# Expert rows of the last three steps added by marking matrices in numbers that differ per token tile, two more tiles read between the last two scatters

## The chip, the cores and the metric

The kernel runs on one core of a Trainium2 chip. A core has TensorE (matrix products, written PE in the profile, its weight loads PEld), VectorE (DVE), ScalarE (ACT), GpSimd (POOL) and SyncE (SP, which here issues most DMAs), and 16 DMA engines that all queues share. The metric is the device time of one execution in microseconds, lower is better.

## What is computed

One decoder layer on 1024 tokens of width 1024: a normalised and modulated input, two attention parts, an output projection, then a mixture of 32 experts in 4 groups, each token going to two experts of one group, and a last normalisation. Only the end matters here:

```python
hid = jax.nn.silu(jnp.dot(h, w_gate[e])) * jnp.dot(h, w_up[e])
y = y + gates[:, e:e + 1] * jnp.dot(hid, w_down[e])      # for every expert e
...
x = x + gate_m[:, None] * y
return rms_norm(x, g_final)
```

## The kernel before

**Expert steps.** Tokens chosen by experts are put on lists, and 20 steps (`NSTEP`) take 128 list entries each. In a step GpSimd gathers the 128 rows (`gather`, L753 on), TensorE turns them, multiplies them with the gate, up and down weights, and VectorE writes the weighted result rows into one of five buffers `held` (`ev_y`). GpSimd then scatters them (`scatter`, issued at L767) to the DRAM tensor `expert_rows` (`y_dram` in the code). It has two rows for each token, one for each of its two experts; one of the pair also carries the token's residual row. A list entry with a negative destination isn't written.

**Late steps.** The last three steps, 17, 18 and 19, are late (`NLATE`, `LATE` = 17). Of their rows, those of the tokens of tiles 0, 1 and 2 (`AHEAD`; a tile is 128 tokens) are not scattered: `late_dst` sets their destination to -1. They are added on TensorE instead. For each of these three tiles and each late step there is a marking matrix (`marks`, 9 of 128 by 128, made by VectorE in expert steps 3 to 11 by comparing `iota_tok` with a column of `late_tok`): a one where list entry and token meet. `add_into` (L2222) multiplies it with the rows still held in `held` and adds into two PSUM banks of the tile; a last product with the identity adds the tile's rows that came by way of DRAM. One product of this kind, marking or identity, covers two halves of 512 columns; it is called a block below. So before, a tile of the three has three marking blocks and one identity block. Since tiles 0 to 2 may miss rows, SyncE first writes zeros to their rows of `expert_rows` (L550), early in the kernel.

**The tail.** SyncE reads both rows of each token back, two DMAs of 512 KB a tile (`expert_rows`, L617). Tiles 0, 1 and 2 are read when scatters 0 to 16 have landed. Tiles 3 to 7 (`read`) are read when all have (`rows_out`, set by GpSimd). VectorE adds the two halves: the early sums of tiles 0 to 2 at L1685, the others in `combine` (L1691), called sum 3 to sum 7. ScalarE squares the whole row of a tile and sums it (L1080, called square), out of PSUM for the tiles of `mixed` and out of SBUF for the others; GpSimd adds a small number (L826) and raises to the power -1/2 (L827); VectorE scales the tile by that and the final gain (`finish`, L1700, called scaling); SyncE stores it (L664). ScalarE, GpSimd and the stores follow the order `last`, tile 0, 3, 4, 1, 5, 6, 2, 7; VectorE's order is written out by hand at the end of its program.

Every engine executes its own instructions in the order in which they are written, and waits at semaphores. So an instruction that waits holds all that stands behind it on its engine.

Of the kernel before, what the change touches and what calls it, by code (L numbers as in the profile page):

```python
# [11 lines left out]
ALU = mybir.AluOpType  # L12
# [53 lines left out]
def hybrid_layer(nc, x, c, w_ada, b_ada, g_attn, w_in, g_kv, w_uk, w_uv, lam_q1, lam_k1, lam_q2, lam_k2,  # L66
# [88 lines left out]
    with ctx:  # L155
# [153 lines left out]
        def dist(t):  # L309
# [86 lines left out]
        late_tok = logits[:, :, :].rearrange("p t n -> p (t n)")[:, 2 * NT + 5 * T + NLATE:2 * NT + 5 * T + NLATE * (1 + AHEAD)].rearrange(  # L396
            "p (i j) -> p i j", j=NLATE)
# [63 lines left out]
        def scattered(b):  # L461

            return len(range(b, LATE, 2))
# [14 lines left out]
        def _(sp):  # L478
# [140 lines left out]
            for n in range(NSTEP + 1):  # L619
# [4 lines left out]
                if n >= 1:  # L624
# [16 lines left out]
            with sp.If(n_ov > 0):  # L641
# [12 lines left out]
                sp.wait_ge(yg_ahead, 64 * AHEAD)  # L654
# [14 lines left out]
        def _(pool):  # L669
# [132 lines left out]
            pool.wait_ge(yg_ahead, 32 * AHEAD)  # L802
# [5 lines left out]
            with pool.If(n_ov > 0):  # L808
# [3 lines left out]
                pool.wait_ge(y_last, 16 * NLATE)  # L812
# [8 lines left out]
            pool.wait_ge(y_last, 16 * NLATE)  # L821
# [9 lines left out]
        def _(act):  # L831
# [253 lines left out]
        def _(dve):  # L1085
# [566 lines left out]
            for n in range(NSTEP):  # L1652
# [9 lines left out]
                if 3 <= n < 3 + NLATE * AHEAD:  # L1662
# [593 lines left out]
```

## Time and profile before

| | us |
|---|---|
| median of 3 runs | 997.08 |
| lowest, highest | 996.19, 998.7 |
| the profiled execution | 995.87 |
| its span, first to last instruction | 994.1 |

| engine | busy us | share of the span |
|---|---|---|
| TensorE | 947.6 | 95% |
| VectorE | 630.1 | 63% |
| ScalarE | 398.3 | 40% |
| GpSimd | 120.3 | 12% |

The profile is of one execution. Times in its rows are counted from the start of the span. A row's busy time is that of the instruction, and the bracket behind it says how long its engine was idle before it and what ended that. The shares are averages over stages that are limited by different things: attention by TensorE, the expert steps by TensorE and the DMA engines together, the last 30 us by neither for their whole length. TensorE's granted clock was 0.992 of full speed over the span and 1.00 in the tail for as long as TensorE was busy there.

### The profile page before, as it was taken

What the parts mean: (1) busy time and instruction counts of PE and PEld (TensorE: products, weight loads), DVE (VectorE), ACT (ScalarE), POOL (GpSimd) and SP (SyncE); (2) the same over time, 40 slices, a digit from 0 to 9 for tenths busy, and PEclk for the clock granted to TensorE, in tenths of its full rate; (3) what the DMA queues carried; (4) which work ended last, traced back from release to release, by engine and by line L of the source; (5) the groups of instructions that cost most, each with busy time, mean ns of one, the idle gap of its engine ahead of it and who ended that gap; (6) DMA issues with size and microseconds to landing.
All of it is one profiled execution on the core that took longest, in us unless ns stands there. A gap on an engine that the chain in (4) does not pass through costs nothing.

```text
span 994.1 us, 15197 instructions
## 1 busy us (share of the span) xinstructions
PE 947.6 (95%) x5400; PEld 520.1 (52%) x5400; DVE 630.1 (63%) x1670; ACT 398.3 (40%) x901; POOL 120.3 (12%) x221
## 2 busy tenths in 40 slices
PE   3899999999999999999999999999899999999895
PEld 2455476444446856667776555555634433344342
DVE  3378646999999799887777423345724444444356
ACT  6131134676671188877668412121211221111103
POOL 2101000000005711110000000000111111111114
PEclk9899999999999999999999999999999999999998
DMA  9998100101103100040000410059899999999979
GB/s 324 328 358 298 43 22 22 44 21 43 43 22 107 69 1 1 2 171 23 2 2 1 156 57 37 27 212 404 312 411 421 393 423 420 420 420 421 420 307 372
DMA packets 70093, 188.37 MB, mean 189 GB/s; under 512 B 10280, under 2 KB 37216, under 8 KB 57728
## 3 DMA queue, kind: packets, MB, share of 16 engines
q1 hardware_dynamic: 61888, 169.48, 44.6%
q0 software_dynamic: 5760, 16.33, 4.2%
q10 hardware_dynamic: 2368, 1.57, 0.5%
q8 instruction: 44, 0.72, 0.3%
q14 instruction: 33, 0.27, 0.1%
HBM read 169.98 MB, written 22.04 MB: 193 GB/s over the span
## 4 chain that ended last, share of the span: by engine, by line
PE 53%; DVE 20%; DMA 16%; issue 6%; POOL 3%; ACT 1%; SPq 0%; DVEq 0%; POOLq 0%; ACTq 0%
DMA expert_rows<-HT,SC 12%; PE PS L2018 11%; DVE BIAS L1222 8%; PE PS L1911 6%; PE PS L2148 5%; PE PS L1954 5%; PE PS L1976 4%; PE PS L1872 3%; PE PS L2171 3%; PE PS L1824 3%; PE PS L1971 2%; DVE X L1286 2%; PE PS L1849 2%; PE PS L1789 2%; DMA HT<-h_rows,SC 2%
## 5 line engine op out<-in xcount | busy, mean ns | idle before, releaser
L1824 PE MATMUL PS<-HT,X 128*128 128x512 f32 x384 | 168.8, 593 | 0.0
L1824 PEld LDWEIGHTS PS<-HT,X 128*128 128x128 f32 x384 | 72.5, 190 | 92.4 <-issue 92.2
L936 ACT ACTIVATE X<-X,nmx 128x128 f32<-128x128 f32 (+7 forms) x128 | 98.4, 770 | 51.7 <-DVE nmx L1286 51.4
L2018 PE MATMUL PS<-QKV,HT 128*128 128x512 f32 x256 | 113.7, 597 | 0.0
L1222 DVE TENSOR_SCALAR_CACHE_REDUCE BIAS<-SC,W 128x384 f32<-128x384 f32 (+3 forms) x128 | 96.4, 810 | 1.1
L2148 PE MATMUL PS<-QKV,HT 128*32 128x512 f32 (+1 forms) x528 | 91.9, 594 | 2.8 <-ACT HT L1034 1.2
L919 ACT ACTIVATE X<-SC,W 128x896 f32<-128x896 f32 x64 | 69.6, 1088 | 43.1 <-DVE W L1210 43.1
L1594 DVE TENSOR_TENSOR HT<-PS,HT 128x256 f32<-128x256 f32 x20 | 8.5, 425 | 123.3 <-ACT HT L1042 123.3
L1911 PE MATMUL PS<-QKV 64*128 64x512 f32 (+3 forms) x384 | 79.0, 517 | 1.6 <-DVE nmx L1286 1.1
L2018 PEld LDWEIGHTS PS<-QKV,HT 128*128 128x128 f32 x256 | 47.4, 190 | 53.7 <-issue 53.6
L1954 PE MATMUL PS<-ident,X 128*128 128x128 f32 x432 | 63.2, 279 | 2.2 <-DVE X L1304 2.1
L1042 ACT ACTIVATE HT<-PS 128x256 f32<-128x256 f32 x20 | 7.7, 383 | 132.2 <-PE PS L2148 125.5
L1286 DVE CUSTOM_DVE_ANT_0 X<-PS,R 128x128 f32<-128x128 f32 (+7 forms) x80 | 50.8, 674 | 14.6 <-PE PS L1911 8.6
L2148 PE MATMUL PS<-SC,HT 128*32 128x512 f32 (+1 forms) x160 | 56.4, 593 | 0.0
L1286 DVE CUSTOM_DVE_ANT_0 X<-PS,SC 128x1024 f32<-128x1024 f32 (+5 forms) x48 | 42.0, 887 | 17.9 <-PE PS L1911 17.8
L1954 PEld LDWEIGHTS PS<-ident,X 128*128 128x128 f32 x432 | 47.3, 141 | 11.4 <-issue 8.6
L1911 PEld LDWEIGHTS PS<-QKV 64*128 64x128 f32 x384 | 31.6, 185 | 27.8 <-issue 20.6
L2148 PEld LDWEIGHTS PS<-QKV,HT 128*32 128x32 f32 (+1 forms) x528 | 24.6, 111 | 36.9 <-issue 34.0
L760 POOL DMA_INDIRECT HT<-h_rows,SC x20 | 20.6, 1029 | 188.9 <-DMA expert_rows<-HT,SC 132.2
L1114 DVE SCALAR_TENSOR_TENSOR QKV<-QKV,cact 128x512 f32<-128x512 f32 x56 | 42.1, 752 | 2.0
L1971 PEld LDWEIGHTS PS<-QKV,HT 128*128 128x128 f32 x288 | 34.5, 191 | 16.6 <-issue 9.2
L2148 PE MATMUL PS<-X,HT 128*32 128x512 f32 (+1 forms) x112 | 42.3, 593 | 0.0
(335 smaller groups left out, 1590.4 us busy)
## 6 DMA issues: line engine op xcount, KB each, us to landing
QKV<-in_w_down_dram SPq DMA_DIRECT2D x20, 1024.0 KB, 26.4
QKV<-in_w_gate_dram SPq DMA_DIRECT2D x19, 1024.0 KB
QKV<-in_w_up_dram SPq DMA_DIRECT2D x19, 1024.0 KB
QKV<-in_w_ada_dram SPq DMA_DIRECT2D x8, 2048.0 KB, 12.7
QKV<-in_w_ada_dram SPq DMA_DIRECT2D x8, 1024.0 KB, 12.5
X<-in_w_in_dram SPq DMA_DIRECT2D x16, 512.0 KB, 3.8
X<-in_w_down_dram SPq DMA_DIRECT2D x8, 1024.0 KB
W<-in_w_gate_dram SPq DMA_DIRECT2D x5, 1024.0 KB
```

What stands on the lines that cost most here:

```text
L919: act.activation(RL[:, n % 2, 0:w], SC[:, sc_off[t]:sc_off[t] + w], ACT.Sign, bias=tk[:, 4, i:i + 1].bitcast(F32), scale=-1.0, accum_out=c ...
L936: act.activation(sc, sc, ACT.Exp, bias=nmx[:, i % 4, m:m + 1], scale=-1.0, accum_out=rs[:, i, m:m + 1]).then_inc(exp_done, 1)
L1114: link(dve.scalar_tensor_tensor(out=w[:, 0, :], in0=w[:, j, :], scalar=cact[:, j:j + 1], in1=w[:, 0, :], op0=ALU.mult, op1=ALU.add))
L1222: dve.tensor_scalar(BIAS[:, i % 3, 0:w], SC[:, sc_off[t]:sc_off[t] + w], thr.bitcast(F32)[:, i:i + 1], 0.0, ALU.is_lt, ALU.add, accum_out= ...
L1286: dve.tensor_tensor_reduce(sc_buf[i % 4][:, m, 0:w], PS[:, 2 * m:2 * m + 2, :].rearrange("p a n -> p (a n)")[:, BANK * n:BANK * n + w], aw ...
L1824: end = pe.matmul(PS[:, 2 * b + half, :], WS[:, b, j, :], HT[:, j, BANK * half:BANK * (half + 1)], start=(j == 0), stop=(j == KC - 1))
L1911: end = pe.matmul(PS[:, 2 * m + n + c0 // BANK, 0:c1 - c0], QKV[rows_m, q0:q0 + P], QKV[rows_m, k0 + c0:k0 + c1], start=True, stop=True)
L1954: end = pe.transpose(PS[:, 4 + g % 2, c0:c0 + P], sc_buf[i % 4][:, m, P * b:P * (b + 1)], ident[:, :])
L1971: end = pe.matmul(PS[:, 6 + h % 2, slot], turned_at(i)[:, g % 4, P * (b - b0):P * (b - b0 + 1)], vf[:, u * S + P * b:u * S + P * (b + 1)], ...
L1976: end = pe.matmul(PS[DH * m:DH * (m + 1), 6 + h % 2, slot], vd[:, b, v0:v0 + DH], turned_at(i)[:, g % 4, c0:c0 + P], start=(b == 0), stop= ...
L2018: end = pe.matmul(PS[:, n % 4, :], HT[:, k, P * (n // 2):P * (n // 2 + 1)], wo[:, k, BANK * (n % 2):BANK * (n % 2 + 1)], start=(k == 0), s ...
L2148: end = pe.matmul(PS[at, 2 + b, :], hgT[b][:, P * c_ + at.start:P * c_ + at.stop], WGU[w][:, c_, :, :], start=(c_ == 0), stop=(c_ == KC - 1))
```

## The change

The three late steps are no longer treated alike. `first_late` = (0, 1, 1, 2, 2) says for tiles 0 to 4 from which late step on their rows are added by marking matrices. Tile 0 has three matrices, tiles 1 and 2 have two, tiles 3 and 4 have one: nine in all, as before. The rows that a matrix no longer covers are scattered: step 17 now leaves out tile 0 alone, step 18 tiles 0 to 2, step 19 tiles 0 to 4. What is read when changes with it: tile 0 after scatter 16, tiles 1 and 2 after scatter 17, tiles 3 and 4 after scatter 18, tiles 5 to 7 after scatter 19. Tiles 3 and 4 are now summed by VectorE first and then enter PSUM through an identity block, and are squared and scaled from PSUM. There are four pairs of banks for five tiles, so tile 4 reuses those of tile 0 and waits until tile 0 is scaled. Five tiles are zeroed at the start. The order of the tail on ScalarE, GpSimd and the stores is tile 0, 5, 1, 3, 6, 4, 7, 2.

```diff
-        AHEAD, NLATE = 3, 3
+        AHEAD, NLATE, PATCHED = 3, 3, 5
+        first_late = (0, 1, 1, 2, 2)
         LATE = NSTEP - NLATE
         read = (3, 4, 5, 6, 7)
-        last = (0, 3, 4, 1, 5, 6, 2, 7)
-        mixed = (0, 1, 2)
+        last = (0, 5, 1, 3, 6, 4, 7, 2)
+        mixed = (0, 1, 3, 4, 2)
...
-        marks = [mark_room[NLATE * i:NLATE * (i + 1)] for i in range(AHEAD)]
+        mark_of = [(i, j) for i in range(PATCHED) for j in range(first_late[i], NLATE)]
+        marks = {at: room for at, room in zip(mark_of, mark_room)}
+        tok_col = [mark_of.index((i, first_late[i])) for i in range(PATCHED)]
+        tiles_of = [sum(1 for f in first_late if f <= j) for j in range(NLATE)]
+        mix_banks = [2 * (i % 4) for i in range(PATCHED)]
...
-            for t in range(AHEAD):
+            for t in range(PATCHED):
                 for k in range(2):
                     row = S * k + P * t
                     sp.dma_start(y_dram[row:row + P, :], zero_rows).then_inc(yg_ahead, 16)
...
                     if n == LATE:
                         for b in range(2):
-                            sp.wait_ge(y_out[b], 16 * scattered(b))
+                            sp.wait_ge(y_out[b], 16 * len(range(b, LATE, 2)))
                         for t in range(AHEAD):
-                            expert_rows(t, yg_ahead)
+                            if first_late[t] == 0:
+                                expert_rows(t, yg_ahead)
+                    if n == LATE + 1:
+                        sp.wait_ge(y_out[1], 16 * scattered(1))
+                        for t in range(AHEAD):
+                            if first_late[t] == 1:
+                                expert_rows(t, yg_ahead)
...
             sp.sem_inc(tables_set, 1)
+            sp.wait_ge(y_out[0], 16 * scattered(0))
+            for t in range(AHEAD, PATCHED):
+                expert_rows(t, yg_in[read.index(t)])
             sp.wait_ge(rows_out, 1)
-            for i, t in enumerate(read):
-                expert_rows(t, yg_in[i])
+            for t in range(PATCHED, T):
+                expert_rows(t, yg_in[read.index(t)])
...
             def scatter(n):
 
                 pool.wait_ge(y_sb, 2 * n + 2)
+                if LATE <= n < NSTEP - 1:
+                    pool.wait_ge(y_out[n % 2], 16 * (n // 2))
...
-            link(dve.tensor_scalar(late_dst, PS[:, 2, LATE:NSTEP], P * AHEAD + 0.5, None, ALU.is_ge))
+            for j in range(NLATE):
+                link(dve.tensor_scalar(late_dst[:, j:j + 1], PS[:, 2, LATE + j:LATE + j + 1], P * tiles_of[j] + 0.5, None,
+                                       ALU.is_ge))
...
-            link(dve.tensor_copy(late_tok[:, 0, :], PS[:, 2, LATE:NSTEP]))
-            for i in range(1, AHEAD):
-                link(dve.tensor_scalar(late_tok[:, i, :], PS[:, 2, LATE:NSTEP], float(-P * i), None, ALU.add))
+            for i, f in enumerate(first_late):
+                link(dve.tensor_scalar(late_tok[:, tok_col[i]:tok_col[i] + NLATE - f], PS[:, 2, LATE + f:NSTEP], float(-P * i),
+                                       None, ALU.add))
...
             finish(0)
             combine(3)
             combine(4)
-            finish(3)
             combine(5)
-            finish(4)
+            finish(5)
             finish(1)
             combine(6)
-            finish(5)
+            finish(3)
+            finish(6)
             combine(7)
-            finish(6)
+            finish(4)
+            finish(7)
             finish(2)
-            finish(7)
...
-            for i in range(AHEAD):
-                for j in range(NLATE):
-                    pe.wait_ge(marked, NLATE * i + j + 1)
+            pe.wait_ge(marked, len(mark_of))
+            for t in mixed:
+                if t >= 4:
+                    pe.wait_ge(fin_done, last.index(t - 4) + 1)
+                for j in range(first_late[t], NLATE):
                     pe.wait_ge(y_sb, 2 * (LATE + j + 1))
-                    add_into(i, marks[i][j], held[(LATE + j) % HELD], j == 0, False)
-                pe.wait_ge(marked, NLATE * AHEAD + i + 1)
-                add_into(i, ident[:, :], yg[i][0], False, True).then_inc(mix_ps, 1)
+                    add_into(mix_banks[t], marks[(t, j)], held[(LATE + j) % HELD], j == first_late[t], False)
+                if t < AHEAD:
+                    pe.wait_ge(marked, len(mark_of) + t + 1)
+                else:
+                    pe.wait_ge(cb_done, read.index(t) + 1)
+                add_into(mix_banks[t], ident[:, :], yg[t][0], False, True).then_inc(mix_ps, 1)
```

VectorE at the end of its program, before the change, from scaling 0 on. L1700 is a scaling, L1691 a sum; X holds tiles 0 to 2, QKV tiles 3 to 7, PS is PSUM, yg_in0 to yg_in4 are the landings of tiles 3 to 7:

```order
L1700 SCALAR_TENSOR_TENSOR X<-PS,ss,HT 128x1024 [waits rstd_done,act_in]
L1691 TENSOR_TENSOR QKV<-QKV 128x1024 [waits yg_in0]
L1691 TENSOR_TENSOR QKV<-QKV 128x1024 [waits yg_in1]
L1700 SCALAR_TENSOR_TENSOR QKV<-QKV,ss,HT 128x1024 [waits rstd_done]
L1691 TENSOR_TENSOR QKV<-QKV 128x1024 [waits yg_in2]
L1700 SCALAR_TENSOR_TENSOR QKV<-QKV,ss,HT 128x1024 [waits rstd_done]
L1700 SCALAR_TENSOR_TENSOR X<-PS,ss,HT 128x1024 [waits rstd_done]
L1691 TENSOR_TENSOR QKV<-QKV 128x1024 [waits yg_in3]
L1700 SCALAR_TENSOR_TENSOR QKV<-QKV,ss,HT 128x1024 [waits rstd_done]
L1691 TENSOR_TENSOR QKV<-QKV 128x1024 [waits yg_in4]
L1700 SCALAR_TENSOR_TENSOR QKV<-QKV,ss,HT 128x1024 [waits rstd_done]
```

Two more scalings follow, of tile 2 and tile 7. The same place after the change, up to the scaling of tile 6; here L1717 is a scaling and L1709 a sum:

```order
L1717 SCALAR_TENSOR_TENSOR X<-PS,ss,HT 128x1024 [waits rstd_done,act_in]
L1709 TENSOR_TENSOR QKV<-QKV 128x1024 [waits yg_in0]
L1709 TENSOR_TENSOR QKV<-QKV 128x1024 [waits yg_in1]
L1709 TENSOR_TENSOR QKV<-QKV 128x1024 [waits yg_in2]
L1717 SCALAR_TENSOR_TENSOR QKV<-QKV,ss,HT 128x1024 [waits rstd_done]
L1717 SCALAR_TENSOR_TENSOR X<-PS,ss,HT 128x1024 [waits rstd_done]
L1709 TENSOR_TENSOR QKV<-QKV 128x1024 [waits yg_in3]
L1717 SCALAR_TENSOR_TENSOR QKV<-PS,ss,HT 128x1024 [waits rstd_done]
L1717 SCALAR_TENSOR_TENSOR QKV<-QKV,ss,HT 128x1024 [waits rstd_done]
```

Sum 7 and the scalings of tiles 4, 7 and 2 follow. Sum 5 moved in front of every scaling but that of tile 0, and its scaling stands directly behind it; tile 3 is scaled from PSUM, between sum 6 and the scaling of tile 6.

SyncE's queue from the last weight load to the first store, before the change (L450 is a weight load, L617 a read of a tile, L664 a store; the branch that is taken only when lists overflow is left out):

```order
L450 DMA QKV<-in_w_down_dram 128x2048
L617 DMA X<-expert_rows 128x1024 [waits dn_ps,y_out0,gu_ps,y_out1]
L617 DMA X<-expert_rows 128x1024 x5
...
L617 DMA QKV<-expert_rows 128x1024 [waits rows_out]
L617 DMA QKV<-expert_rows 128x1024 x9
L664 DMA out_0_dram<-X 128x1024 [waits fin_done]
```

And after it, where L622 is a read of a tile and L678 a store:

```order
L622 DMA X<-expert_rows 128x1024 [waits dn_ps,y_out0,gu_ps,y_out1]
L622 DMA X<-expert_rows 128x1024
L622 DMA X<-expert_rows 128x1024 [waits y_out1,dn_ps,gu_ps]
L622 DMA X<-expert_rows 128x1024 x3
...
L622 DMA QKV<-expert_rows 128x1024 [waits y_out0]
L622 DMA QKV<-expert_rows 128x1024 x3
L622 DMA QKV<-expert_rows 128x1024 [waits rows_out]
L622 DMA QKV<-expert_rows 128x1024 x5
L678 DMA out_0_dram<-X 128x1024 [waits fin_done]
```

Sixteen reads in two groups became sixteen reads in four: two, four, four and six.

## Rows read from the trace of the kernel before

**Rows 1.** Chain of waits, 930 to 995: start us, us, what.

```profile
963.82 3.35 DMA expert_rows<-HT,SC
...
967.32 0.33 SPq L617
...
968.64 6.20 DMA QKV<-expert_rows
```

**Rows 2.** Windows of 3 us: busy us of each engine, PEclk, DMA share, GB/s.

```profile
963.00:966.00 3.00, 3.00 (x8) 1.33 (x7) 2.15 (x3) 0.00 (x0) 0.97 (x1) 1.00 0.21 75
```

**Rows 3.** Timeline of the tail: start us, us, engine, line, operation [idle before].

```profile
963.89 3.50 DVE L1685 TENSOR_TENSOR X<-X 128x1024 f32<-128x1024 f32 x3 [0.85 <-issue]
...
969.57 0.19 POOL L826 TENSOR_TENSOR ss<-ss,eps_row 128x1 f32<-128x1 f32 x1 [4.77 <-ACT HT L1080]
...
970.50 1.28 DVE L1700 SCALAR_TENSOR_TENSOR X<-PS,ss,HT 128x1024 f32<-128x1024 f32 x1 [3.11 <-POOL ss L827]
...
972.30 1.23 DVE L1691 TENSOR_TENSOR QKV<-QKV 128x1024 f32<-128x1024 f32 x1 [0.52 <-DMA QKV<-expert_rows]
...
973.56 1.06 ACT L1080 ACTIVATE HT<-QKV 128x1024 f32<-128x1024 f32 x1 [4.08 <-DVE QKV L1691]
...
974.79 0.19 POOL L826 TENSOR_TENSOR ss<-ss,eps_row 128x1 f32<-128x1 f32 x1 [4.39 <-ACT HT L1080]
974.87 1.23 DVE L1691 TENSOR_TENSOR QKV<-QKV 128x1024 f32<-128x1024 f32 x1 [1.33 <-DMA QKV<-expert_rows]
...
975.06 1.45 POOL L827 TENSOR_TENSOR ss<-ss,neghalf 128x1 f32<-128x1 f32 x1
...
976.54 1.28 DVE L1700 SCALAR_TENSOR_TENSOR QKV<-QKV,ss,HT 128x1024 f32<-128x1024 f32 x1 [0.45 <-POOL ss L827]
...
981.12 1.28 DVE L1700 SCALAR_TENSOR_TENSOR X<-PS,ss,HT 128x1024 f32<-128x1024 f32 x1 [0.44 <-POOL ss L827]
981.32 0.54 POOL L827 TENSOR_TENSOR ss<-ss,neghalf 128x1 f32<-128x1 f32 x1
982.32 1.22 DVE L1691 TENSOR_TENSOR QKV<-QKV 128x1024 f32<-128x1024 f32 x1
...
984.65 1.22 DVE L1691 TENSOR_TENSOR QKV<-QKV 128x1024 f32<-128x1024 f32 x1
...
984.79 1.12 POOL L826 TENSOR_TENSOR ss<-ss,eps_row 128x1 f32<-128x1 f32 x1 [2.94 <-ACT HT L1080]
...
990.80 0.33 SPq L664 DMA_DIRECT2D out_dram<-QKV  x1
```

**Rows 4.** Timeline of TensorE, its marking blocks and the first identity block.

```profile
961.30 5.31 PE L2222 MATMUL PS<-HT,BIAS 128*128 128x512 f32 x12
...
966.45 1.88 PE L2222 MATMUL PS<-X,ident 128*128 128x512 f32 x4
```

**Rows 5.** Timeline of GpSimd, scatters 17 and 18.

```profile
948.38 0.97 POOL L767 DMA_INDIRECT expert_rows<-HT,SC  x1 [13.06 <-DVE HT L1606]
959.24 0.97 POOL L767 DMA_INDIRECT expert_rows<-HT,SC  x1 [9.89 <-DVE HT L1606]
```

**Rows 6.** The tile expert_rows at 948.3 to 948.45, scatter 17 alone.

```profile
DMA to landing us min/median/max: 7.7/7.7/7.7
```

**Rows 7.** The tile expert_rows at 959 to 960, scatter 18 alone.

```profile
DMA to landing us min/median/max: 5.0/5.0/5.0
```

**Rows 8.** The tile expert_rows, SyncE, 948 to 952: the six early reads.

```profile
L617 SPq DMA_DIRECT2D X<-expert_rows x6: 319/458/509, 948.5 to 951.1; - x6
...
DMA to landing us min/median/max: 6.0/8.1/11.0
```

**Rows 9.** The tile expert_rows, SyncE, 969.6 to 970: both reads of tile 5.

```profile
DMA to landing us min/median/max: 7.0/7.3/7.5
```

**Rows 10.** Timeline of VectorE before the first expert step, 713 to 716.

```profile
715.74 0.41 DVE L1616 TENSOR_SCALAR HT<-PS,gm,modc 128x128 f32<-128x128 f32 x1 [1.91 <-PE PS L2135]
```

**Rows 11.** The tile expert_rows over the span: the zeroing stores.

```profile
L550 SPq DMA_DIRECT2D expert_rows<-W x6: 433/1188/1596, 317.3 to 322.7; - x6
```

More of the change, by code:

```diff
@@ L461, in scattered @@
         def scattered(b):
-            return len(range(b, LATE, 2))
+            return len(range(b, NSTEP - 1, 2))
         def uses(b):
@@ L653, in _ @@
                 sp.wait_ge(rows_out, 1)
-                sp.wait_ge(yg_ahead, 64 * AHEAD)
+                sp.wait_ge(yg_ahead, 32 * PATCHED + 32 * AHEAD)
                 for t in range(AHEAD):
@@ L769, in scatter @@
                                         bounds_check=2 * S - 1, oob_is_err=False
-                                        ).then_inc(y_out[n % 2] if n < LATE else y_last, 16)
+                                        ).then_inc(y_out[n % 2] if n < NSTEP - 1 else y_last, 16)
             def overflow_rows(n, i, b):
@@ L801, in _ @@
             pool.wait_ge(route_done, 2)
-            pool.wait_ge(yg_ahead, 32 * AHEAD)
+            pool.wait_ge(yg_ahead, 32 * PATCHED)
             for n in range(NSTEP):
@@ L811, in _ @@
                     pool.wait_ge(y_out[b], 16 * scattered(b))
-                pool.wait_ge(y_last, 16 * NLATE)
+                pool.wait_ge(y_last, 16)
                 with pool.Fori(0, NOV // 2) as i:
@@ L820, in _ @@
                 pool.wait_ge(y_out[b], 16 * scattered(b))
-            pool.wait_ge(y_last, 16 * NLATE)
+            pool.wait_ge(y_last, 16)
             pool.sem_inc(rows_out, 1)
@@ L1073, in _ @@
                     act.wait_ge(mix_ps, i + 1)
-                    whole = PS[:, 2 * i:2 * i + 2, :].rearrange("p a n -> p (a n)")
+                    whole = PS[:, mix_banks[t]:mix_banks[t] + 2, :].rearrange("p a n -> p (a n)")
                 else:
@@ L1661, in _ @@
                     dve.wait_ge(tables_set, 2 * NE + 2)
-                if 3 <= n < 3 + NLATE * AHEAD:
-                    i, j = divmod(n - 3, NLATE)
-                    dve.tensor_scalar(marks[i][j], iota_tok, late_tok[:, i, j:j + 1], None, ALU.is_equal).then_inc(marked, 1)
+                if 3 <= n < 3 + len(mark_of):
+                    dve.tensor_scalar(marks[mark_of[n - 3]], iota_tok, late_tok[:, n - 3:n - 2], None,
+                                      ALU.is_equal).then_inc(marked, 1)
             dve.wait_ge(route_done, 2)
@@ L1669, in _ @@
                     dve.wait_ge(y_out[b], 16 * scattered(b))
-                dve.wait_ge(y_last, 16 * NLATE)
+                dve.wait_ge(y_last, 16)
                 place_overflow()
@@ L1682, in _ @@
             dve.wait_ge(tables_set, 2 * NE + 3)
-            dve.wait_ge(yg_ahead, 64 * AHEAD)
+            dve.wait_ge(yg_ahead, 32 * PATCHED + 32 * AHEAD)
             for t in range(AHEAD):
@@ L1696, in finish @@
                 if t in mixed:
-                    i = mixed.index(t)
-                    whole = PS[:, 2 * i:2 * i + 2, :].rearrange("p a n -> p (a n)")
+                    whole = PS[:, mix_banks[t]:mix_banks[t] + 2, :].rearrange("p a n -> p (a n)")
                 dve.wait_ge(rstd_done, rstd_out + last.index(t) + 1)
@@ L2217, in _, with add_into @@
                             down_proj(n, over(b), [(b, 0, 4)], [(b, came(DNS))])
-            def add_into(i, stationary, rows, start, stop):
+            def add_into(bank, stationary, rows, start, stop):
                 for h in range(2):
-                    end = pe.matmul(PS[:, 2 * i + h, :], stationary, rows[:, BANK * h:BANK * (h + 1)], start=start,
+                    end = pe.matmul(PS[:, bank + h, :], stationary, rows[:, BANK * h:BANK * (h + 1)], start=start,
                                      stop=stop)
                 return end
-            for i in range(AHEAD):
-                for j in range(NLATE):
-                    pe.wait_ge(marked, NLATE * i + j + 1)
-                    pe.wait_ge(y_sb, 2 * (LATE + j + 1))
-                    add_into(i, marks[i][j], held[(LATE + j) % HELD], j == 0, False)
-                pe.wait_ge(marked, NLATE * AHEAD + i + 1)
-                add_into(i, ident[:, :], yg[i][0], False, True).then_inc(mix_ps, 1)
+            pe.wait_ge(marked, len(mark_of))
[3 more added lines that the diff above has]
+                for j in range(first_late[t], NLATE):
+                    pe.wait_ge(y_sb, 2 * (LATE + j + 1))
+                    add_into(mix_banks[t], marks[(t, j)], held[(LATE + j) % HELD], j == first_late[t], False)
[4 more added lines that the diff above has]
+                add_into(mix_banks[t], ident[:, :], yg[t][0], False, True).then_inc(mix_ps, 1)
 _INS = ["x", "c", "w_ada", "b_ada", "g_attn", "w_in", "g_kv", "w_uk", "w_uv", "lam_q1", "lam_k1", "lam_q2", "lam_k2",
```

4 lines of the change are left out of this document (2 added, 2 removed).

## Prediction

> **What bounds the kernel now.** I read the page first, then the chain of waits, the DMA by windows, and the timeline of the last 35 us. Only the tail is touched in a way that can move the end, so the reader should see three things there. First, the last scatter (step 19) is issued at 963.82 and its landing, 3.35 us later, starts all ten reads of tiles 3 to 7; the read issued at 968.64 lands 6.20 us later and only then does tile 4's sum start [rows 1]. Second, the DMA engines are nearly idle at 963 to 966 (share 0.21) [rows 2]: that hole is where the change puts four reads. Third, around 981 to 985 VectorE runs without a gap: sums (1.22 us each) and final scalings (1.28 us) stand back to back, and the last store is issued at 990.80 [rows 3]. TensorE's adding, 12 blocks that begin at 961.30 [rows 4], ends at about 982, long before the end. So the reads bound the tail until about 977, VectorE with its partners after that.
>
> **What the change removes: waiting for tiles 3 and 4.** Scatters 17, 18, 19 landed 7.7, 5.0 and 3.4 us after their issues at 948.38, 959.24 and 963.82, so at 956.1, 964.2 and 967.2 [rows 1, 5, 6, 7]. Tiles 1 and 2 are now read when scatter 17 has landed. At 956.1 at the latest, four reads start; by the spacing of the ten reads before (first issue 967.32, the fourth, of 968.64, landed at 974.84, which is 7.5 us) they land by 963.6, where the six early reads of before ended at 951.1 + 11.0 = 962.1 [rows 1, 8]. VectorE's first early sum starts at 963.89 anyway, takes 1.17 us, and TensorE wants it at 966.45 [rows 3, 4], so 1.4 us are spare: between 0 and 0.5 us of delay, and I take none.
> The queue in front of scatter 18 empties those 1.5 us later, so it lands not at 964.2 but between 964.2 and 965.7; I take 965.2, nearer to the late end because the load of the final gain and the scatter itself share that queue time. Four reads are then issued from 965.2, against 967.32 before: 2.1 us earlier, not the 4.6 us that lie between the two scatters. The engines have the hole of [rows 2] for them, and tiles 5 to 7 follow in the same stream. Tile 5's second read, issued at 969.9, landed 7.5 us later at 977.4, 10.1 us after the first issue [rows 9]; now 965.2 + 10.1 = 975.3.
>
> **What it adds on TensorE.** Nine marking blocks stay nine; identity blocks grow from 3 to 5. A block is 4 matmul instructions of 0.43 us (12 from 961.30 to 966.45) [rows 4], 1.72 us. Two more are 3.4 us; 14 blocks from 961.30 end at 985.4. The order is now tile 0, 1, 3, 4, 2, and the new waits (the sum of tile 3, the first scaled tile, the sum of tile 4) are over by 974, before TensorE comes to them at 975 or later. Behind the last block come square, power and scaling: 985.4 + 0.2 + 1.2 + 0.9 + 1.3 = 989.0. That is a floor, 1.8 us under 990.8.
>
> **What it moves: the order on VectorE, ScalarE and GpSimd.** This is the term that decides. Before, each scaling of a summed tile had at least one other VectorE instruction between it and its sum; now scaling 5 stands right behind sum 5, scaling 1 behind it, and so on. Durations: a sum lets its square start 1.25 us after its own start, the square feeds GpSimd 1.23 us later (973.56 to 974.79), and GpSimd's two small instructions need 0.93 us when nothing holds them (969.57 to scaling 0 at 970.50) [rows 3]. They are held: the power that started at 975.06 took 1.45 us and ended 0.41 us after the sum that began at 974.87; the one at 981.32, beside a scaling that reads PSUM, took only 0.54 us; the addition at 984.79, beside a sum, 1.12 us [rows 3]. Back to back, a scaling costs 1.20 (981.12 to 982.32), a sum and a scaling together 2.33 (982.32 to 984.65), so a sum 1.13 [rows 3].
> With sum 5 starting at S: it ends S+1.2; scaling 5 can start only at S+1.25+1.23+0.93 = S+3.4, so VectorE idles 2.2 us. Power 1 is held by scaling 5, so scaling 1 starts at S+5.1. Sum 6 S+6.3; scaling 3 (from PSUM) S+7.5, ends S+8.7; square 6 is behind sum 6, so scaling 6 starts S+6.3+3.4 = S+9.7, idle 1.0. Sum 7 S+10.9. Power 4 is held by scaling 6 and sum 7, so scaling 4 starts S+12.6; scaling 7 at S+10.9+3.4 = S+14.3; power 2 is held by scaling 7, so scaling 2 starts S+16.3 and ends S+17.6. Tiles 6 and 7 have landed long before their sums.
> S itself: scaling 0 is unchanged at 970.50 [rows 3], sums 3 and 4 follow at 971.7 and 972.8, so S is at least 974.0 by VectorE; by the reads it is 975.3. The end on VectorE is 975.3 + 17.6 = 992.9, against 990.8: **+2.1 us**. The gain of 2.1 us at the reads is spent by some 5 us of new idle places and by a chain of four tiles behind sum 6. With S = 974.0 it is 991.6, +0.8 us.
> The Trainium skill, SBUF — State Buffer, section A bandwidth-pool intuition that's wrong, says that the held engine goes on some 115 ns after VectorE's end, where the power here ended 0.41 us after it. By the page the sum would be about 0.3 us smaller.
>
> **Edits that cost nothing.** Four more short VectorE instructions before the first expert step, 0.2 us each or 0.8 us: VectorE waited 1.91 us there for TensorE, up to 715.74 [rows 10]; without that cover they cost 0.8 us. Four more zeroing stores of 512 KB at about 323: six took 317.3 to 322.7 to issue [rows 11], so some 5 us more of SyncE's queue, whose next entry waits for the end of all scores, hundreds of us away. GpSimd's new waits before scatters 17 and 18 are for scatters 15 and 16, which SyncE also awaits before its early reads; those began right after 948.38, so the waits are over when they come. What is queued behind them, scatter 19 and the small instructions of the tail, isn't moved.
>
> **Rivals.** (a) *The last scatter is held by the reads in front of it (slower).* The four reads share the DMA engines with scatter 19. For: scatter 17, with six reads beside it, took 7.7 us, scatter 19, alone, 3.4 [rows 1, 6]. If it takes 7.7 now it lands at 971.5, tile 5 follows 5.0 us later (as tile 3 did, 972.30 after 967.32) [rows 1, 3], S = 976.6, the end 994.2: +3.4 us, 1000.5. It costs something from a landing after 970.2, and decides the sign at 0.3% from about 971. Against: its rows flow at about 965 to 966, before the data of reads issued at 965.2, and fewer rows (tiles 5 to 7 only) are written.
> The Trainium skill, DMA: Bandwidth & Descriptors, section Queues, rings and completion order, has each DMA engine take turns between queues packet by packet. By that rule scatter 19 would share with the reads and end nearer this rival.
> (b) *The early reads carry through (faster).* If the idle places do not open, because the squares and powers return faster than the rows say, the end falls to TensorE's floor: 989.0, -1.8 us, 995.3. For it speaks that VectorE's busy work is no larger than before. Against it: 3.4 us from sum to scaling is seen in the trace (972.30 and 976.54, 4.2 with a held power) [rows 3].
> (c) *The change doesn't do what it says.* Scatter 18, behind the later reads of tiles 1 and 2, lands no earlier than scatter 19 does. Then S is 977.4 as before and the end 995.0, +4.2 us, 1001.3. It needs a latency of 8 us where 5.0 was seen.
>
> **How the numbers follow.** The profiled execution took 995.87 with a span of 994.1; the median of the runs is 997.08, 1.2 above it, and I add the change to the median: 997.08 + 2.0 = 999.1. A measurement can tell about 0.3%, 3 us, from no change. Chances: forecast, S between 974.0 and 976.1 (+0.8 to +2.9), 0.68; rival (a) 0.18; rival (b) 0.09; rival (c) 0.05. Rival (b) alone stays within 3 us save for a small part, so faster 0.02, same 0.75, slower 0.23. The range runs from +0.1 (the forecast's low end less what a median scatters) to +3.9 us, so 997.2 to 1001.0, and leaves out (b) and (c).
>
> **What would show it.** In the trace after: four reads issued near 965 instead of 967.3; sum 5 near 975.3; VectorE idle some 2 us behind sum 5 with GpSimd as its releaser, and again 1 us before scaling 6; TensorE ending near 985.4 with no wait; the last scaling ending near 993. I am wrong if scatter 19 lands after 970, if the early sums start after 965.2, or if scaling 5 starts less than 3 us after sum 5.

## The result and the profile after

The changed kernel takes 999.97 us (median of 15 runs, 997.89 to 1002.94), the kernel before, run beside it, 995.28 us (15 runs, 990.93 to 998.7). The ratio is 1.0054, 95% interval 1.0041 to 1.0067: 5.3 us slower. A second series of the same kernel, run later beside the kernel before, gave 1.0051 (1.0038 to 1.0064, 5 runs). The profiled execution took 999.74 us with a span of 998.0.

Where the last 35 us begin differs by some microseconds from one execution to the next: TensorE's first marking block starts between 959.2 and 963.5 in the traces kept here, at 959.96 and at 963.49 in two of the changed kernel. So all places in the tail are counted here from that event, at 961.30 before [rows 4] and at 959.96 after. Before, the last store is issued 29.5 us behind it [rows 3], after it 35.0 us behind it. By these two traces that is 5.5 us, so the whole loss lies in this stretch.

The chain of waits of the changed kernel (start us, us, what) answers to [rows 1]:

```profile
957.90 8.53 DMA expert_rows<-HT,SC
...
966.44 0.33 SPq L622
...
969.11 8.13 DMA QKV<-expert_rows
...
977.26 1.24 DVE QKV L1709
...
978.52 1.16 ACT HT L1096 x2
...
993.62 1.28 DVE X L1717
```

It is scatter 18, not scatter 19, that now starts the reads, and it took 8.53 us to land. Scatter 18 before took 5.0 [rows 7].

The DMA engines around the landing of scatter 17, windows of 1 us (busy us of each engine, PEclk, DMA share, GB/s), first of the changed kernel, then a window of before at nearly the same place:

```profile
953.00:954.00 1.00, 1.00 (x12) 0.26 (x8) 0.41 (x2) 0.00 (x0) 0.00 (x0) 1.00 0.76 299
954.00:955.00 1.00, 1.00 (x16) 0.26 (x8) 0.96 (x2) 0.00 (x0) 0.00 (x0) 1.00 0.23 94
955.00:956.00 1.00, 0.95 (x10) 0.31 (x2) 0.83 (x2) 0.02 (x1) 0.00 (x0) 1.00 0.27 86
```

```profile
954.00:955.00 1.00, 1.00 (x16) 0.30 (x12) 0.58 (x2) 0.00 (x0) 0.00 (x0) 1.00 1.03 414
```

The four reads of tiles 1 and 2 wait for scatter 17, and some 2 us of DMA time before them go unused. The answer on the tile expert_rows, SyncE, 952 to 962, shows these four (duration ns min/median/max, first and last start), and what the late ones cost:

```profile
L622 SPq DMA_DIRECT2D X<-expert_rows x4: 320/424/432, 954.7 to 956.0; - x4
...
  DVE X L1703: 4.2, 1
DMA to landing us min/median/max: 3.6/5.2/9.8
```

The last of them landed 9.8 us after its issue, at 965.8; VectorE's early sums stood still for it for 4.2 us. The timeline of the tail answers to [rows 3] and [rows 4] (start us, us, engine, line, operation, idle before):

```profile
956.91 0.35 ACTq L1085 DMA_DIRECT2D HT<-in_g_final_dram  x1
...
957.90 0.97 POOL L783 DMA_INDIRECT expert_rows<-HT,SC  x1 [9.88 <-DVE HT L1622]
...
959.96 5.31 PE L2239 MATMUL PS<-HT,BIAS 128*128 128x512 f32 x12
...
965.90 3.50 DVE L1703 TENSOR_TENSOR X<-X 128x1024 f32<-128x1024 f32 x3 [4.20 <-DMA X<-expert_rows]
966.44 5.68 SPq L622 DMA_DIRECT2D QKV<-expert_rows  x10
...
967.18 2.72 PE L2239 MATMUL PS<-X,ident 128*128 128x512 f32 x4 [1.91 <-DVE X L1703]
...
977.26 1.23 DVE L1709 TENSOR_TENSOR QKV<-QKV 128x1024 f32<-128x1024 f32 x1 [1.33 <-DMA QKV<-expert_rows]
...
980.60 1.28 DVE L1717 SCALAR_TENSOR_TENSOR QKV<-QKV,ss,HT 128x1024 f32<-128x1024 f32 x1 [2.11 <-POOL ss L843]
...
980.96 0.98 POOL L842 TENSOR_TENSOR ss<-ss,eps_row 128x1 f32<-128x1 f32 x1 [0.39 <-ACT HT L1096]
...
982.59 1.28 DVE L1717 SCALAR_TENSOR_TENSOR X<-PS,ss,HT 128x1024 f32<-128x1024 f32 x1 [0.70 <-POOL ss L843]
...
986.15 1.88 PE L2239 MATMUL PS<-X,ident 128*128 128x512 f32 x4
...
987.11 1.28 DVE L1717 SCALAR_TENSOR_TENSOR QKV<-QKV,ss,HT 128x1024 f32<-128x1024 f32 x1 [0.91 <-POOL ss L843]
...
988.31 1.22 DVE L1709 TENSOR_TENSOR QKV<-QKV 128x1024 f32<-128x1024 f32 x1
988.52 1.41 POOL L843 TENSOR_TENSOR ss<-ss,neghalf 128x1 f32<-128x1 f32 x1
...
989.96 1.28 DVE L1717 SCALAR_TENSOR_TENSOR QKV<-PS,ss,HT 128x1024 f32<-128x1024 f32 x1 [0.44 <-POOL ss L843]
...
991.63 1.28 DVE L1717 SCALAR_TENSOR_TENSOR QKV<-QKV,ss,HT 128x1024 f32<-128x1024 f32 x1 [0.38 <-POOL ss L843]
...
993.62 1.28 DVE L1717 SCALAR_TENSOR_TENSOR X<-PS,ss,HT 128x1024 f32<-128x1024 f32 x1 [0.71 <-POOL ss L843]
994.93 0.33 SPq L678 DMA_DIRECT2D out_dram<-X  x1
```

All ten reads of tiles 3 to 7 left in one piece, from 966.44 on: 6.5 us behind the first marking block, where before it was 6.0. Sum 5 started at 977.26, 17.3 us behind it, against 16.4 before. So nothing was gained at the reads; 0.9 us was lost. From the start of sum 5 the last scaling ended 17.6 us later (993.62 + 1.28 - 977.26). TensorE ended at 986.15 + 1.88 = 988.0, off the path.

The same stretch before, sum 5, then the scalings behind it that waited, and the last one:

```profile
977.74 1.22 DVE L1691 TENSOR_TENSOR QKV<-QKV 128x1024 f32<-128x1024 f32 x1
...
979.39 1.28 DVE L1700 SCALAR_TENSOR_TENSOR QKV<-QKV,ss,HT 128x1024 f32<-128x1024 f32 x1 [0.44 <-POOL ss L827]
...
986.57 1.28 DVE L1700 SCALAR_TENSOR_TENSOR QKV<-QKV,ss,HT 128x1024 f32<-128x1024 f32 x1 [0.71 <-POOL ss L827]
...
988.29 1.28 DVE L1700 SCALAR_TENSOR_TENSOR X<-PS,ss,HT 128x1024 f32<-128x1024 f32 x1 [0.44 <-POOL ss L827]
...
989.49 1.27 DVE L1700 SCALAR_TENSOR_TENSOR QKV<-QKV,ss,HT 128x1024 f32<-128x1024 f32 x1
```

That is 13.0 us (989.49 + 1.27 - 977.74). The 4.6 us more and the 0.9 are the loss. The 4.6 us are not all idle time. VectorE's waits behind sum 5 add up to 5.25 us after and to 2.03 before (0.44 each before the scalings of tiles 4, 1 and 2, 0.71 before that of tile 6): 3.2 us more. Some 1.2 us are one scaling more: that of tile 3 stood ahead of sum 5 before, in time in which VectorE would have waited for reads, and stands behind it now.

### The profile page after: what moved, and what is told of

The parts are those of the page before. It is cut to its first block, busy times and chain, and to the rows that moved or that the text cites. A ratio compares the mean times of both kernels' runs of the same rounds, so it can differ in the third digit from the quotient of the medians.

```text
span 998.0 us, 15216 instructions
## 1 busy us (share of the span) xinstructions
PE 952.4 (95%) x5408; PEld 521.2 (52%) x5408; DVE 631.6 (63%) x1674; ACT 398.3 (40%) x901; POOL 118.5 (12%) x221
## 4 chain that ended last, share of the span: by engine, by line
PE 52%; DVE 20%; DMA 17%; issue 6%; SPq 3%; POOL 2%; ACT 1%; POOLq 0%; DVEq 0%; ACTq 0%
DMA expert_rows<-HT,SC 13%; PE PS L2035 11%; DVE BIAS L1238 8%; PE PS L1928 7%; PE PS L2165 5%; PE PS L1971 5%; PE PS L1993 4%; PE PS L1889 3%; PE PS L1841 3%; PE PS L2188 2%; PE PS L1988 2%; SPq L495 2%; DVE X L1302 2%; PE PS L1866 2%; DMA HT<-h_rows,SC 2%
## 5 line engine op out<-in xcount | busy, mean ns | idle before, releaser
L1928 PE MATMUL PS<-QKV 64*128 64x512 f32 (+3 forms) x384 | 81.8, 533 | 1.6 <-DVE nmx L1302 1.1
## 6 DMA issues: line engine op xcount, KB each, us to landing
QKV<-in_w_up_dram SPq DMA_DIRECT2D x19, 1024.0 KB, 17.7
```

Of the source, the lines that this page charges most:

```text
L1928: end = pe.matmul(PS[:, 2 * m + n + c0 // BANK, 0:c1 - c0], QKV[rows_m, q0:q0 + P], QKV[rows_m, k0 + c0:k0 + c1], start=True, stop=True)
```

## The experiments

Two theories stood against each other. **A**: the tail order costs most of it. **B**: the reads do, because tiles 1 and 2 are read late and stand in front of scatter 18. All ratios are to the kernel before on the same chip, with 95% intervals. Changes of order are written as the sequence on VectorE, s for sum, f for scaling.

**The order alone**, put into the kernel before:

```diff
-        last = (0, 3, 4, 1, 5, 6, 2, 7)
+        last = (0, 5, 1, 3, 6, 4, 7, 2)
...
-            f0 s3 s4 f3 s5 f4 f1 s6 f5 s7 f6 f2 f7
+            f0 s3 s4 s5 f5 f1 s6 f3 f6 s7 f4 f7 f2
```

> Kernel before with one edit: the tail order of the changed kernel (tiles 0, 5, 1, 3, 6, 4, 7, 2 on ScalarE, GpSimd and the stores; sum 5 ahead of all scalings but that of tile 0). Reads and marking matrices are those of before, tiles 3 and 4 stay in SBUF. Theory A (the order costs most of the loss): sum 5 starts where it did, about 977.5 to 977.8, and the last scaling ends 17.6 us behind it as in the changed kernel, not 13.0 us behind it as before: slower than before by 4 to 5 us, ratio 1.004 to 1.005. Theory B (the loss comes from the reads of tiles 1 and 2 that start late and hold scatter 18 and TensorE): this kernel has none of that, so ratio 1.000, at most 1 us.

Ratio 1.0042 (1.0027 to 1.0056), 4.2 us. Its timeline, sum 5, scaling 5 and the last scaling (first marking block at 959.28):

```profile
975.75 1.23 DVE L1691 TENSOR_TENSOR QKV<-QKV 128x1024 f32<-128x1024 f32 x1 [1.35 <-DMA QKV<-expert_rows]
...
979.09 1.28 DVE L1700 SCALAR_TENSOR_TENSOR QKV<-QKV,ss,HT 128x1024 f32<-128x1024 f32 x1 [2.11 <-POOL ss L827]
...
992.18 1.28 DVE L1700 SCALAR_TENSOR_TENSOR X<-PS,ss,HT 128x1024 f32<-128x1024 f32 x1 [0.44 <-POOL ss L827]
```

Sum 5 starts where it did before, 16.5 us behind the first block, and the end comes 17.7 us behind sum 5. Theory A holds for some four fifths of the loss.

**The order undone**, in the changed kernel:

```diff
-        last = (0, 5, 1, 3, 6, 4, 7, 2)
+        last = (0, 1, 3, 5, 4, 6, 7, 2)
...
-            f0 s3 s4 s5 f5 f1 s6 f3 f6 s7 f4 f7 f2
+            f0 s3 s4 s5 f1 s6 f3 f5 s7 f4 f6 f7 f2
```

> Changed kernel with another tail order: tiles 0, 1, 3, 5, 4, 6, 7, 2, and on VectorE scaling 0, sums 3, 4, 5, scaling 1, sum 6, scalings 3, 5, sum 7, scalings 4, 6, 7, 2, so that two or three instructions stand between the sum and the scaling of tiles 5 and 6. Reads and matrices as in the changed kernel. Theory A: the last scaling ends about 14 us behind sum 5 instead of 17.6, so some 3.6 us are won back, ratio to before 1.0015 to 1.0025. Theory B: the start of sum 5 and of the reads decides, the order wins under 1 us, ratio 1.0045 to 1.0055.

Ratio 1.0019 (1.0002 to 1.0036), against the 1.0054 of the first series: 3.5 us back. Scatter 18 again took 8.5 us and sum 5 started at 17.0 us, but the end came 13.4 us behind it. Its timeline, sum 5 and the last scaling:

```profile
977.91 1.22 DVE L1709 TENSOR_TENSOR QKV<-QKV 128x1024 f32<-128x1024 f32 x1 [1.33 <-DMA QKV<-expert_rows]
...
990.02 1.28 DVE L1717 SCALAR_TENSOR_TENSOR X<-PS,ss,HT 128x1024 f32<-128x1024 f32 x1 [0.70 <-POOL ss L843]
```

**The load of the gain moved.** In the trace after, this load (512 KB, issued at 956.91) lies between the reads of tile 2 and scatter 18.

```diff
-        gfin = HF[:, 3072:3072 + D]
+        gfin = X[:, 6144:6144 + D]
...
-            act.dma_start(gfin, g_final.partition_broadcast(P)).then_inc(act_in, 16)
...
                     if n == LATE + 1:
+                        sp.dma_start(gfin, g_final.partition_broadcast(P)).then_inc(act_in, 16)
                         sp.wait_ge(y_out[1], 16 * scattered(1))
```

> Changed kernel with the load of the final gain (128 copies of one 4 KB row, 512 KB) issued by SyncE right after the down projection of step 17, into a free part of X, instead of by ScalarE at 956.9 between the reads of tile 2 and scatter 18. It then falls into the hole in which the DMA engines wait for scatter 17. Theory B, fine form (scatter 18 took 8.5 us because reads and this load stand in front of it): scatter 18 lands 1.5 to 3 us earlier, the first of the ten reads goes out before scatter 19 has landed, TensorE no longer waits for the early sums, sum 5 starts 1 to 2.5 us earlier, ratio to before 1.003 to 1.0045. Theory that the load doesn't matter: scatter 18 still takes 8 us or more, ratio 1.005 to 1.006.

Ratio 1.0037 (1.0019 to 1.0056). Scatter 18 took 7.0 us, sum 5 started at 15.0. Repeated beside its control:

> The gain load ahead of the reads of tiles 1 and 2, with the changed kernel's order, beside its control. Expected if the load is worth something: 1 to 2.5 us less than the control. Its two earlier traces differed: scatter 18 took 7.0 us here and 7.8 us with the spread order, sum 5 started at 15.0 and 16.9 us behind the first marking block. If the load is worth nothing, no difference from the control beyond 0.5 us.

Ratio 1.0044 (1.0032 to 1.0057), the control 1.0051 (1.0038 to 1.0064). That is 0.7 us with intervals that overlap for the most part, so with this order the load isn't shown to matter. The trace of this repetition is of little use: TensorE stood still just before the tail (below, in the last section).

The control, the changed kernel once more:

> The changed kernel unaltered, as the control on the same chip as the next three and for a second trace. Expected: ratio 1.004 to 1.0065 again; scatter 18 lands 8 us or more after its issue, no read of tiles 3 and 4 gets far ahead of scatter 19's landing, sum 5 starts 17.0 to 17.5 us behind TensorE's first marking block and the last scaling ends 17.6 us behind that. If the latency of scatter 18 was an accident of one execution, it is 5 to 6.5 us here and sum 5 comes at 14 to 16.

The ratio is the one seen before. Its timeline, the first marking block, sum 5 and the last scaling:

```profile
963.49 5.31 PE L2239 MATMUL PS<-HT,BIAS 128*128 128x512 f32 x12
...
979.09 1.22 DVE L1709 TENSOR_TENSOR QKV<-QKV 128x1024 f32<-128x1024 f32 x1 [1.32 <-DMA QKV<-expert_rows]
...
995.44 1.28 DVE L1717 SCALAR_TENSOR_TENSOR X<-PS,ss,HT 128x1024 f32<-128x1024 f32 x1 [0.70 <-POOL ss L843]
```

Scatter 18 took 7.2 us instead of 8.5, sum 5 came at 15.6 us, the last store 33.3 us behind the first block instead of 35.0. So the size of the reads' part moves by more than 1 us from execution to execution, while the 17.6 us behind sum 5 were there again (979.09 to 996.72). This tail is 3.8 us longer than that of before, where the series has 5.1: a tail of one trace tells the loss to 1 us or so.

**Load and order together:**

> Changed kernel with its reads and matrices, the final gain loaded ahead of the reads of tiles 1 and 2, and the spread tail order. Alone, the gain load gave 1.0037 and the order 1.0019 where the changed kernel has 1.0054. If the two costs lie one behind the other on one chain (landing of scatter 18, then the order behind sum 5), their gains add: 1.0054 - 0.0017 - 0.0035 = 1.0002, and the last scaling ends some 29.0 to 29.6 us behind the first marking block. If they cover each other, it is no better than the order alone: 1.0015 to 1.002.

> Gain load early and spread order, beside the control. The first time the ratio was 0.9991, while the trace of that run had its end 30.9 us behind the first marking block, 1.5 us more than before has. If the gains of order (3.4 us) and load (1 to 2 us) add, 1.000 to 1.0015; the first figure of 0.9991 would then be at the favourable end of its interval. If it was right, 0.9985 to 0.9995.

Ratios 0.9991 (0.9977 to 1.0005) and 1.0000 (0.9988 to 1.0011). The order alone had 1.0019, so the load seems worth 2 to 3 us here, more than the near nothing it showed with the other order. The two answers don't agree, the intervals touch, and what the load is worth stays open, between 0 and 3 us. What is clear is that both cures together bring the kernel back to the time of before, and no further.

**Tiles 1 and 2 read early again**, three marking matrices each:

```diff
-        first_late = (0, 1, 1, 2, 2)
+        first_late = (0, 0, 0, 2, 2)
```

(The two matrices more need room, taken from two tiles that are free by then. That line isn't shown, nor the like one of the last version below.)

> Changed kernel with tiles 1 and 2 put back: three marking matrices each, read right after scatter 16 like tile 0, as before (matrices 3, 3, 3, 1, 1; eleven in all, TensorE two blocks or 3.4 us more). Tiles 3 and 4 are still read after scatter 18. Theory B: scatter 18 lands after about 5.0 us as before, so the reads of tiles 3 and 4 begin some 3 us ahead of the landing of scatter 19 and sum 5 starts at about 12.7 to 13.5 us after TensorE's first marking block (before 16.4, changed kernel 17.3). With the changed kernel's order the end is then 17.6 us behind that, or set by TensorE's 16 blocks: 27.5 + 3.6 = 31.1 us after the first block, against 29.5 before: ratio 1.001 to 1.002. If the reads in flight hold scatter 19 instead (latency 5 us or more instead of 3.4), sum 5 comes 1.5 to 3 us later than that and the ratio is 1.002 to 1.004.

Ratio 1.0027 (1.0012 to 1.0041). This one shows what holds scatter 18. The answers on the tile expert_rows for scatter 18 and then scatter 19 of this kernel:

```profile
L783 POOL DMA_INDIRECT expert_rows<-HT,SC x1: 977/977/977, 960.3 to 960.3; - x1
...
DMA to landing us min/median/max: 4.7/4.7/4.7
```

```profile
L783 POOL DMA_INDIRECT expert_rows<-HT,SC x1: 977/977/977, 964.9 to 964.9; - x1
...
DMA to landing us min/median/max: 4.6/4.6/4.6
```

Without the late reads scatter 18 lands after 4.7 us, the reads of tiles 3 and 4 go out 2.7 us behind the first block, and sum 5 starts at 13.6. Scatter 19, with four reads beside it, takes 4.6 us instead of 3.4: 1.2 us more. The end, 31.3 us behind the first block, is both 17.6 us behind sum 5 and where TensorE's 16 blocks put it. Which of the two holds it was the next question:

> Changed kernel with both cures at once: tiles 1 and 2 read after scatter 16 again (matrices 3, 3, 3, 1, 1; 16 TensorE blocks), and the spread tail order 0, 1, 3, 5, 4, 6, 7, 2. The experiment without the spread order had sum 5 at 13.6 us behind the first marking block and the end of the last scaling at 31.3. If the chain behind sum 5 is what ends last, it is now some 14 us long and the end comes at 27 to 28: ratio 0.9975 to 0.999. If TensorE's floor (16 blocks of 1.72 us, then square, power and scaling of tile 2: 27.5 + 3.6 to 3.8 = 31.1 to 31.3) is what ends last, the new order wins nothing: ratio 1.0015 to 1.003 as without it.

Ratio 1.0016 (1.0005 to 1.0028), the end at 31.0 us. The timeline, TensorE's last block, the square and the scaling of tile 2:

```profile
986.84 1.88 PE L2239 MATMUL PS<-X,ident 128*128 128x512 f32 x4
988.75 1.02 ACT L1096 ACTIVATE HT<-PS 128x1024 f32<-128x1024 f32 x1 [3.27 <-PE PS L2239]
...
990.79 1.28 DVE L1717 SCALAR_TENSOR_TENSOR X<-PS,ss,HT 128x1024 f32<-128x1024 f32 x1 [2.26 <-POOL ss L843]
```

ScalarE waits for TensorE now, and VectorE by way of ScalarE and GpSimd. More rows by matrix means more blocks, and TensorE becomes the end: with 16 blocks it is 31.0 us behind the first one, where before everything was over at 29.5.

**A version meant to beat both:** only tile 3 gets a matrix of its own (14 blocks), tiles 0 to 2 as before, and a tail order with room behind each sum.

```diff
-        AHEAD, NLATE, PATCHED = 3, 3, 5
-        first_late = (0, 1, 1, 2, 2)
+        AHEAD, NLATE, PATCHED = 3, 3, 4
+        first_late = (0, 0, 0, 2)
-        last = (0, 5, 1, 3, 6, 4, 7, 2)
-        mixed = (0, 1, 3, 4, 2)
+        last = (0, 4, 1, 5, 6, 3, 7, 2)
+        mixed = (0, 1, 3, 2)
...
-            f0 s3 s4 s5 f5 f1 s6 f3 f6 s7 f4 f7 f2
+            f0 s3 s4 s5 f4 s6 f1 f5 s7 f6 f3 f7 f2
```

> A version meant to beat both: tiles 0 to 2 exactly as in the kernel before (three matrices each, read after scatter 16), only tile 3 added with one matrix and read after scatter 18 (matrices 3, 3, 3, 1; 14 TensorE blocks as in the changed kernel), tail order 0, 4, 1, 5, 6, 3, 7, 2 with one or more VectorE instructions between each sum and its scaling. Counted from TensorE's first marking block (before: sum 5 at 16.4, last scaling ends at 29.5): tile 3's reads start at about 2.9, those of tiles 4 to 7 at 6.0 to 6.5, sum 5 starts at about 13.5 to 14.5, TensorE's adding ends at 24.1, and the last scaling, of tile 2, ends at 27.8 if the reads and the order are what costs in the changed kernel: ratio 0.9982, or 0.998 to 0.9995. If reads in front of scatter 19 hold it (4.6 us with four of them, 3.4 with none), about 0.5 us later. If neither theory holds, 1.001 or more.

> The best version so far (tile 3 alone with one matrix and read after scatter 18) with the gain loaded by SyncE right after the down projection of step 17, in front of the six early reads, instead of by ScalarE while scatter 18 is under way. If that load is part of what holds scatter 18 (5.8 us in the version's trace), scatter 18 lands after about 5 us, tile 3's reads start 1 us earlier, but tiles 4 to 7 still wait for scatter 19, and the end is near TensorE's floor of 27.7: ratio 0.998 to 0.9993. If the early reads are then later by the 1.2 us that the load takes and hold scatter 18 as much, no gain: 0.9993 to 1.000.

The second is the first with the gain loaded by SyncE ahead of the six early reads. Ratios 0.9993 (0.9982 to 1.0004) for both. Neither is told apart from the kernel before. The first ended at 28.9 us, 1.1 us behind its estimate; in its trace scatter 18 took 5.8 us and sum 5 started at 15.4, not at 14. That the one follows from the other isn't shown: in the trace of the second, scatter 18 took 5.2 us and tile 3's reads left 0.6 us sooner, but scatter 19 then took 5.2 us instead of 3.3, sum 5 started at 16.0 and the last store was issued at 29.2.

The tails, counted from TensorE's first marking block to the issue of the last store, beside the measured ratio. Each is of one trace. They agree with the ratios to 1.3 us or better, save for "changed, both": 1.5 us longer than before by its trace, 0.9 us faster by its series. The repetition with the early gain load is left out, because its first block came late and ran slowly (last section).

| kernel | scatter 18, us to landing | sum 5 starts | last store | ratio |
|---|---|---|---|---|
| before | 5.0 | 16.4 | 29.5 | 1 |
| changed | 8.5 | 17.3 | 35.0 | 1.0054 |
| changed, second series | 7.2 | 15.6 | 33.3 | 1.0051 |
| before, new order alone | 5.9 | 16.5 | 34.2 | 1.0042 |
| changed, spread order | 8.5 | 17.0 | 30.5 | 1.0019 |
| changed, gain load early | 7.0 | 15.0 | 32.7 | 1.0037 |
| changed, both | 7.8 | 16.9 | 31.0 | 0.9991 |
| changed, both, again | 7.1 | 16.0 | 29.7 | 1.0000 |
| early reads kept | 4.7 | 13.6 | 31.3 | 1.0027 |
| early reads kept, spread order | 4.9 | 14.3 | 31.0 | 1.0016 |
| tile 3 alone | 5.8 | 15.4 | 28.9 | 0.9993 |
| tile 3 alone, gain load early | 5.2 | 16.0 | 29.2 | 0.9993 |

## Why the prediction was right or wrong

The forecast was +2 us, with three quarters on no change that can be told; the measured 5.3 us is slower beyond that bound. That the median of 999.97 lies inside the range of 997.2 to 1001.0 is luck: the kernel before measured 995.28 in the longer series and not the 997.08 from which the sum was made, and 997.08 + 5.3 = 1002.4 would lie outside. The direction was right, the size was 3 us short, and the case nearest to what came had been given 0.05.

**The chain behind sum 5: right, and it is the main cost.** The prediction laid out each square, power and scaling from sum 5 on and got 17.6 us. The two traces of the changed kernel have 17.6, the order alone 17.7. Places and reasons also came as written: VectorE idle 2.11 us before scaling 5 with GpSimd as the releaser, 0.91 us before scaling 6, power 4 held for 1.41 us. On the margin, GpSimd's addition before scaling 1 was the one that was held (0.98 us), not the power; scaling 1 came 5.3 us behind the start of sum 5 instead of 5.1, and the total of 17.6 stood. That one of these microseconds is a scaling that changed places, and not idle time, the text doesn't say ("some 5 us of new idle places"): new are 3.2 us.

**The Trainium skill's figure for the held engine**, 115 ns (SBUF — State Buffer, section A bandwidth-pool intuition that's wrong), was said to make this sum 0.3 us smaller. It does not follow: the figure says when the held engine goes on, and the 0.41 us of the text are when its instruction ends. The trace has both. A held power ended 0.40 us behind VectorE's (988.52 + 1.41 = 989.93, sum 7 ended at 988.31 + 1.22 = 989.53), a held addition 0.06 us behind it (980.96 + 0.98 = 981.94, scaling 5 ended at 980.60 + 1.28 = 981.88).

**The landing of scatter 18: the step that failed.** The text put it at 965.2 in the time of before, 3.9 us behind the first marking block; it came at 6.5 and 5.2. The term is the queue in front of it, which was to empty 1.5 us later and to cost scatter 18 1.0 us. Before the change it landed 2.9 us behind the block; the queue cost it 3.5 us in the first trace and 2.2 in the second. The start of the four reads came as written or sooner (5.3 and 6.0 us ahead of the first block, forecast 5.2), but they were given the 7.5 us that four reads take on free DMA engines. The last of them landed 11.1 us after the first was issued in the first trace, with 9.8 us of its own. In the second trace they took 8.3 us and landed as forecast, 2.3 us behind the block, and scatter 18 was late all the same. The four reads had been moved 5.5 to 6.5 us later, past a hole of 2 us or more in which the DMA engines were mostly idle, and then the four reads, the load and the scatter, up to 3 MB, met in one place. With the early reads kept, scatter 18 took 4.7 and 4.9 us: it is the moved reads that held it. For sum 5 the forecast meant 14.0 us behind the first block (975.3 - 961.3). It came at 17.3 in the first trace, 3.3 us late, which is the whole miss, and at 15.6 in the second.

**TensorE's cover of the early sums: wrong in one trace of two.** The text had "between 0 and 0.5 us of delay", and took none. In the first trace the sums came 3.3 us later than before (5.9 instead of 2.6 us behind the first block, which is past its own sign of being wrong), TensorE waited 1.91 us and scaling 0 came at 12.1 instead of 9.2 us. It cost nothing in the end, since sums 4 and 5 waited for their reads anyway. In the second trace, where the reads landed in time, there was no such wait.

**TensorE's floor: right.** 14 blocks ended off the path, 24.2 us behind the first block in the second trace, as forecast (24.1), and 28.1 in the first, after the wait and at a lower clock (last section). The estimate for 16 blocks in the expectations, 31.1 us, was met by 31.0 and 31.3.

**Edits that cost nothing: nothing speaks against it.** The changed kernel with both cures has all of them and measured 0.9991 and 1.0000.

**Rivals.** (a), scatter 19 held by the reads: real but small, 1.1 to 1.2 us where the reads stand beside it (early reads kept, 4.6 and 4.5 us). In the changed kernel it took 4.4 us in the first trace, with scatter 18 and the late reads still under way, and 3.2 in the second; it landed at 6.9 and 5.7 us, when reads were being issued already. (b) did not come; VectorE's idle places opened. (c), scatter 18 lands no earlier than scatter 19 did: the first trace is this case (6.5 us, scatter 19 before 5.9), the second lies between it and the forecast, with 0.9 of the 2.1 us gained at the first read. Its price was given as 4.2 us, its chance as 0.05 with the reason that it needs a latency of 8 us where 5.0 was seen. But the change moves 2 MB of reads in front of that very scatter, so the old latency was no evidence; scatter 17, with reads beside it, had taken 7.7 [rows 6].

## What to carry to other kernels

A read that must wait for a later event does not only start later: it loses the idle DMA time before that event and lands on whatever is issued next, so price the transfer behind it with the new queue, not with its old latency. When a tile's work goes through three engines and comes back, its last step needs other instructions of the first engine in between; with two to four between them the stretch behind sum 5 was 13.4 us, with none or one 17.6, for the same ten instructions. And work that is done while VectorE would wait for reads, like the scaling of tile 3 before the change, costs its 1.2 us once it is moved behind them. Work moved onto TensorE has a floor of its own: count its blocks to the end before giving it more.

## What the runs showed of the hardware

A scatter's latency went with what was queued around it. Scatter 19 took 4.5 to 5.2 us with two or four 512 KB reads issued within the next microsecond, and 2.9 to 3.5 without, save for 4.4 in two traces. Scatter 18 took 4.7 to 5.9 us at the tail of six earlier reads and 7.0 to 8.5 behind four later ones. Scatter 16 took 14.0 us behind the last weight loads. Why two kernels with the same queue differ by 1 us, as before and the order alone do (5.0 and 5.9), stays open.

A wait of TensorE of 1.91 us was followed by a granted clock of 0.55 of full speed for the 3 us from 969 to 972, though TensorE was busy all that time (windows of 3 us of the changed kernel):

```profile
966.00:969.00 3.00, 1.82 (x4) 0.84 (x5) 3.00 (x3) 0.00 (x0) 0.00 (x0) 0.88 0.45 137
969.00:972.00 3.00, 3.00 (x6) 1.21 (x5) 0.40 (x1) 1.11 (x2) 0.76 (x2) 0.55 0.93 373
```

Waits of 1.76 and 1.64 us at the same place (spread order; both cures) were not followed by it: the granted clock stayed at 1.00.

In one execution (the repetition with the early gain load) TensorE stood still for 4.6 us between the last expert step and the first marking block, where the profile names no wait. The DMA engines were full until 961. The granted clock fell to 0.55 in the window of 960 to 961, while TensorE stood still, and its first twelve matmuls then ran at the lower of its two clock levels (1.2 GHz, granted 0.50) and took 7.53 us instead of 5.31:

```profile
962.62 7.53 PE L2239 MATMUL PS<-HT,BIAS 128*128 128x512 f32 x12 [4.60 <-issue]
```

Each of these kernels has a branch at that place. The answers on DMA (`--dma`) show one packet of 8 KB on an instruction queue, q14, between 961.0 and 961.8 of this trace, and one more between 961.8 and 962.7, where the matmuls begin. In the trace of before, that queue's packet lies between 953 and 954, 7 to 8 us ahead of the first block. That TensorE waited for its instructions would fit, but it isn't shown: it is one trace, and the rows don't say whose instructions they are.
